# Moving the norm's root from the input to the products, and splitting stage borders into column halves

## The chip, the cores and the metric
One Trainium2 chip, one core. The kernel is one program on one core, with an order of instructions written out by hand for TensorE (matrix products), VectorE, ScalarE and GpSimd, and SyncE for the transfers of the weights. The metric is the device time of one execution in microseconds.

## The reference
Three transformer layers over a sequence of 256 tokens with D = 1024, all in float32. Cut to what matters here:

```
rmsnorm(x, g) = x * rsqrt(mean(x*x) + EPS) * g
layer a:  x += attention(rope(q), rope(k), v) @ w_o   with q, k, v = split(rmsnorm(x) @ w_qkv)
          x += conv_ffn(rmsnorm(x))                   u = h @ w_up; u = conv_b + sum of 3 taps of u; (silu(gate)*val) @ w_down
layer b:  k, v from rmsnorm(x, kv_norm), q from rmsnorm(x, attn_norm[1]), a window of 128 and sinks; then conv_ffn again
          x = rmsnorm(x, final_norm)
layer 2:  xn = rmsnorm(x, norm_mix_pre); proj = xn @ w_in
          a gated delta rule over 8 heads, behind 4-tap convolutions and silus of q, k, v
          retention over 4 heads, behind a rotation
          x += rmsnorm((sigmoid(gate_a)*ya + sigmoid(gate_b)*yb) @ w_out)
          x += rmsnorm(square(relu(rmsnorm(x) @ w_up)) @ w_down)
```

All of it is computed to float32 precision.

## The kernel before
**Weights.** All weights come as 200 units of 1 MB (128 partitions x 2048 values), in the order in which they are used. SyncE loads unit u into one of four raw slots (`load_weights`, L247), as soon as VectorE has finished with unit u-4. ScalarE rounds the unit to a high part in two halves (`hi`, L253, copies at L258 and L259), and VectorE subtracts to get the low part (`lo`, L262, L266 and L268). A product is three matmuls, high x high, low x high, high x low (`three`, L275 to L277). Each engine takes its instructions in the order in which they were written, and the calls of `hi()` and `lo()` stand between the other operations of ScalarE and VectorE at places chosen by hand. `features` (L290) makes a unit's products with features on the partitions, 48 matmuls in four steps; `tokens` (L305) has tokens there.

**Norms.** At every stage border x (256 tokens in two tiles, 1024 columns) gets its residual in four chunks of 128x512 (`residual_dve`, L421, L428), ScalarE sums the squares (`mean_squares_act`, L355), GpSimd makes the root, ScalarE and VectorE scale a tile each into `wide` (L375, L380), TensorE turns it in sixteen 128x128 transposes (L387, `normed_pe`), and ScalarE and VectorE make the high and low part of h from the banks, with the gain (`turn_act` L399, `turn_dve` L411). Then the next stage's products can begin.

**Attention.** `rot_dve` rotates q and k from their bank with the cos and sin tables (L566, L567, L570). In `attn_b` all queries use bank 0, and a query's products wait until the one before is rotated.

**FFN.** 11 laps. A lap has two units up and one down. Per up unit ScalarE applies the newest tap from the bank (`newest_act`, L964) and VectorE the two older taps, four operations (`conv_dve`, L984); then silu (L970), the product (L995), and the high and low part of the gated result (`gate_act` L976, `gate_dve` L999), which the down unit needs (`down_pe`, accumulating in four banks). The scripts of the two engines are `act` (L1001) and `dve` (L1015).

**Delta heads.** 7 laps of `delta_pe`, `delta_act`, `delta_dve`. While TensorE makes the four units of head n = hd+1, head hd's 128x128 inverse is built in six levels: TensorE's `level_a_pe` (L1345), a copy by ScalarE (`level_a_act`, L1351), TensorE's `level_b_pe` (L1356, L1359), a subtraction by VectorE (L1365). `newest_act(n, s)` (L1200) and `older_dve(n, s, back)` (L1208) are the convolution. ScalarE's order around the third level is:

```
newest_act(n, 1)
hi()
level_a_act(hd, 3)
```

and VectorE's `sides_dve(hd)`, `older_dve(n, 1, 1)`, `level_b_dve(hd, 3)`.

**End.** After w_out, `add_normed_dve` (L2117, L2120) adds the normed mix to x, chunk by chunk, and a norm as above leads to the MLP, eight laps of four units.

## Time and profile before

| | us |
|---|---|
| median of 3 runs | 1484.54 |
| lowest, highest | 1483.83, 1486.79 |
| profiled execution, its own time | 1486.77 |
| its span | 1485.2 |
| TensorE busy | 1363.4 |
| VectorE busy | 902.6 |
| ScalarE busy | 726.9 |

All times in the rows are from the profiled execution, counted from the start of its span. The mean granted TensorE clock is 0.972 of full speed. In a timeline row the first number is the start, the second the busy time of the group, and "x4" says how many instructions it holds; the bracket at its end is the time that the engine stood idle before it, and what ended that.

### The profile page before, as it was taken

The numbers are of one execution on the slowest core, as the hardware profiler recorded it, in microseconds if no ns is written. First come the engines' busy times: TensorE is split into PE (matmuls) and PEld (weight loads), VectorE is DVE, ScalarE is ACT, GpSimd is POOL, SyncE is SP. The second block draws the span as 40 slices with busy tenths as digits, with TensorE's granted clock in tenths as the row PEclk, the third lists the DMA queues.
The fourth block names the chain that finished last, engine by engine and source line by source line (L and its number), as shares of the span: only waits on it lengthen the run. The fifth ranks groups of instructions, "written<-read, shape, count | busy, mean of one in ns | idle before, by whom it ended". The sixth has DMA issues, their size and how long they took to land.

```text
span 1485.2 us, 22970 instructions
## 1 busy us (share of the span) xinstructions
PE 1363.4 (92%) x9480; PEld 1241.6 (84%) x9480; DVE 902.6 (61%) x1424; ACT 726.9 (49%) x1260; POOL 88.7 (6%) x145
## 2 busy tenths in 40 slices
PE   6999999987689999978999999979999999699997
PEld 5987999976668999968888888868898877598986
DVE  6765766666557766667666666753557544565553
ACT  6545545554447445557545554543334342553442
POOL 0000000000000000001221221220000000000000
PEclk9999999999899999989999999999999999899999
DMA  8342555433223554433233233223544443365540
GB/s 301 135 167 102 187 202 192 171 142 114 86 85 142 192 203 174 170 139 141 87 114 111 88 115 114 87 84 133 208 151 160 177 168 136 117 248 183 193 142 29
DMA packets 33656, 218.70 MB, mean 147 GB/s; under 512 B 4368, under 2 KB 6032, under 8 KB 7952
## 3 DMA queue, kind: packets, MB, share of 16 engines
q1 hardware_dynamic: 29376, 210.87, 39.2%
q10 hardware_dynamic: 4176, 6.36, 1.3%
q8 instruction: 75, 1.23, 0.3%
q14 instruction: 29, 0.24, 0.1%
HBM read 216.17 MB, written 1.05 MB: 146 GB/s over the span
## 4 chain that ended last, share of the span: by engine, by line
PE 81%; DVE 10%; ACT 5%; issue 2%; POOL 1%; DMA 0%; ACTq 0%; DVEq 0%; SPq 0%; POOLq 0%
PE bank L275 24%; PE bank L276 23%; PE bank L277 23%; DVE sb_w_lo L268 2%; DVE sb_w_lo L266 2%; PE bank L1345 1%; PE bank L1356 1%; ACT sb_w_hi L258 1%; DVE sb_d_xt L1365 1%; PE bank L387 1%; DVE sb_wide L1208 1%; PE bank L643 1%; PE bank L1359 1%; PE bank L592 1%; ACT sb_wide L362 1%
## 5 line engine op out<-in xcount | busy, mean ns | idle before, releaser
L275 PE MATMUL bank<-sb_h_hi,sb_w_hi 128*128 128x256 f32 x1536 | 445.5, 290 | 18.8 <-DVE sb_attn_b_q L570 17.7
L276 PE MATMUL bank<-sb_h_lo,sb_w_hi 128*128 128x256 f32 x1536 | 434.5, 283 | 0.0
L277 PE MATMUL bank<-sb_h_hi,sb_w_lo 128*128 128x256 f32 x1536 | 434.3, 283 | 0.0
L266 DVE TENSOR_TENSOR sb_w_lo<-sb_raw,sb_w_hi 128x1024 fp32r<-128x1024 f32 x200 | 244.3, 1222 | 193.1 <-ACT sb_w_hi L258 192.6
L275 PEld LDWEIGHTS bank<-sb_h_hi,sb_w_hi 128*128 128x128 f32 x1536 | 293.0, 191 | 25.1 <-DVE sb_attn_b_q L570 18.3
L276 PEld LDWEIGHTS bank<-sb_h_lo,sb_w_hi 128*128 128x128 f32 x1536 | 292.9, 191 | 2.7 <-issue 1.4
L277 PEld LDWEIGHTS bank<-sb_h_hi,sb_w_lo 128*128 128x128 f32 x1536 | 292.7, 191 | 0.0
L268 DVE TENSOR_TENSOR sb_w_lo<-sb_raw,sb_w_hi 128x1024 fp32r<-128x1024 f32 x200 | 248.0, 1240 | 0.0
L258 ACT CAST sb_w_hi<-sb_raw 128x1024 fp32r<-128x1024 f32 x200 | 210.3, 1052 | 69.2 <-PE bank L277 69.2
L259 ACT CAST sb_w_hi<-sb_raw 128x1024 fp32r<-128x1024 f32 x200 | 210.8, 1054 | 0.0
L275 PE MATMUL bank<-sb_w_hi,sb_h_hi 128*128 128x256 f32 (+1 forms) x544 | 173.2, 318 | 5.6 <-DVE sb_wide L1208 3.0
L276 PE MATMUL bank<-sb_w_lo,sb_h_hi 128*128 128x256 f32 (+1 forms) x544 | 164.8, 303 | 0.0
L277 PE MATMUL bank<-sb_w_hi,sb_h_lo 128*128 128x256 f32 (+1 forms) x544 | 164.3, 302 | 0.0
L275 PEld LDWEIGHTS bank<-sb_w_hi,sb_h_hi 128*128 128x128 f32 x544 | 103.9, 191 | 11.1 <-DVE sb_wide L1208 3.2
L277 PEld LDWEIGHTS bank<-sb_w_hi,sb_h_lo 128*128 128x128 f32 x544 | 103.6, 190 | 4.6
L276 PEld LDWEIGHTS bank<-sb_w_lo,sb_h_hi 128*128 128x128 f32 x544 | 104.0, 191 | 4.0 <-issue 0.5
L275 PE MATMUL bank<-sb_w_hi,sb_mid_hi 128*128 128x512 f32 (+1 forms) x208 | 82.7, 398 | 6.4 <-DVE sb_attn_b_q L570 6.4
L276 PE MATMUL bank<-sb_w_lo,sb_mid_hi 128*128 128x512 f32 (+1 forms) x208 | 80.8, 388 | 0.0
L277 PE MATMUL bank<-sb_w_hi,sb_mid_lo 128*128 128x512 f32 (+1 forms) x208 | 80.8, 388 | 0.0
L387 PE MATMUL bank<-sb_ident,sb_wide 128*128 128x128 f32 x112 | 23.5, 395 | 43.7 <-ACT sb_wide L375 31.9
L387 PEld LDWEIGHTS bank<-sb_ident,sb_wide 128*128 128x128 f32 x112 | 21.2, 211 | 46.1 <-ACT sb_wide L375 34.1
L984 DVE SCALAR_TENSOR_TENSOR sb_ffn_b_cv<-bank,sb_conv,sb_ffn_b_cv 128x255 f32<-128x255 f32 (+1 forms) x88 | 38.3, 477 | 35.1 <-ACT sb_ffn_b_cv L964 34.4
(310 smaller groups left out, 2001.1 us busy)
## 6 DMA issues: line engine op xcount, KB each, us to landing
sb_raw<-stream SPq DMA_DIRECT2D x200, 1024.0 KB, 4.8
sb_row<-rows ACTq DMA_DIRECT2D x3, 512.0 KB, 4.4
sb_x<-x SPq DMA_DIRECT2D x2, 512.0 KB, 5.4
sb_norm_b<-norm_b ACTq DMA_DIRECT2D x4, 256.0 KB, 3.5
out<-sb_x ACTq DMA_DIRECT2D x4, 256.0 KB, 2.0
sb_retain<-retain ACTq DMA_DIRECT2D x1, 768.0 KB, 4.3
sb_levels<-levels ACTq DMA_DIRECT2D x1, 448.0 KB, 3.3
sb_masks<-mask_full ACTq DMA_DIRECT2D x1, 192.0 KB, 5.3
```

The lines of the kernel that those rows point to most:

```text
L258: A.copy(w_hi[:, b, 0:HALF], raw[:, b, 0:HALF]).then_inc(hi_done, 1)
L259: A.copy(w_hi[:, b, HALF:UNIT], raw[:, b, HALF:UNIT]).then_inc(hi_done, 1)
L266: V.tensor_tensor(w_lo[:, b, 0:HALF], raw[:, b, 0:HALF], w_hi[:, b, 0:HALF].bitcast(F32), ALU.subtract)
L268: V.tensor_tensor(w_lo[:, b, HALF:UNIT], raw[:, b, HALF:UNIT], w_hi[:, b, HALF:UNIT].bitcast(F32), ALU.subtract).then_inc(lo_done, 1)
L275: T.matmul(out_ap, l_hi, r_hi, start=start, stop=False, **kw)
L276: T.matmul(out_ap, l_hi, r_lo, start=False, stop=False, **kw)
L277: return T.matmul(out_ap, l_lo, r_hi, start=False, stop=stop, **kw)
L362: ins = A.activation(chunk(junk, t, n), chunk(x, t, n), ACT.Square, scale=D ** -0.5, accum_out=small[:, 2 * t + n:2 * t + n + 1])
L387: mm = T.transpose(bank[TURN_BANKS[b]][:, c:c + P], wide[:, t, k * P:(k + 1) * P], ident[:])
L592: mm = T.matmul(bank[3 + r][:, c0:c0 + w], self.q[rows, a_, q0:q0 + P], self.k[rows, a_, k0:k0 + w], start=False, stop=a_ == 1, skip_group ...
L643: mm = T.transpose(bank[3 + r][:, c * P:(c + 1) * P], self.sc[:, r, c * P:(c + 1) * P], ident[:])
L984: ins = V.scalar_tensor_tensor(self.cv[:, y, back:S], bank[(0 if j else 2) + s][:, i * S:(i + 1) * S - back], cw[:, y, 2 - back:3 - back], ...
```

## The change
The new kernel turns x as it is, without its norm. The gain is applied where the high and low parts are made; the root r of each token is applied later, to the products. For that a row of the roots is made on every partition: `row_pe` multiplies the broadcast root with the identity (two matmuls), and `row_act` copies the result to `r_row`. Where tokens lie on the partitions the root is a scale of the activation (v, silu_z, the sigmoids); in attention the cos and sin tables are multiplied by the row; in the FFN and in the delta heads each unit's product is multiplied by the row into SBUF ahead of the convolution.

x is turned in two column halves (`turn_x_pe`), the first of them between the last products of the stage before, and the next stage's first two units are interleaved with the second half in `first_two`. The raw slots are three instead of four; the parts of the weights keep four. The queries of attn_b alternate banks 0 and 1, as do the up banks and the gate parts of the FFN and the MLP. In the delta entry the final norm and the pre-norm of the next layer are one root. The core of the diff:

```
-SLOTS = 4
+SLOTS, RAW = 4, 3
...
+                if u >= RAW:
+                    Q.wait_ge(lo_done, u - RAW + 1)
...
+        def row_pe(b, m, c0=4):
+            T.wait_ge(rstd, m + 1)
+            for t in range(NT):
+                mm = T.matmul(bank[b][:, t * P:(t + 1) * P], small[:, c0 + t:c0 + t + 1].to_broadcast([P, P]), ident[:], ...
+        def row_act(b, n):
+            A.wait_ge(row_mm, n + 1)
+            A.copy(r_row[:], bank[b][:, 0:S]).then_inc(row_done, 1)
+        def first_two(u0, b0, u1, b1, fresh, nx, banks, acts=None, second=None):
+            features(u0, b0, 0, acts, fresh)
+            features(u0, b0, 2, acts, fresh)
+            turn_x_pe(nx, 1, banks)
+            second(u1, b1, 0, acts, fresh)
+            second(u1, b1, 2, acts, fresh)
+            features(u0, b0, 1, acts, fresh)
+            features(u0, b0, 3, acts, fresh)
+            second(u1, b1, 1, acts, fresh)
+            second(u1, b1, 3, acts, fresh)
...
         def attn_b_pe(at):
-                T.wait_ge(rot_done, 2 * GROUPS + (1 + g if g else 0))
-                features(q, 0, 0)
+                b, fr = g % 2, 12 if g == 0 else None
+                if g:
+                    T.wait_ge(rot_done, at.rots(g - 2, "q") if o >= 0 else at.rots(0, "k"))
+                features(q, b, 0, fresh=fr)
...
+        def enter_act(mm0, nx, targets, turned_in, h0=0):
+            turn_act(mm0, targets[:1], HALVES[0], turned_in)
+            mean_squares_act(nx, wide)
+            turn_act(mm0, targets[:1], HALVES[1], turned_in)
...
+            def scale_dve(self, j, s):
+                e = 2 * (self.l0 + j) + s
+                V.wait_ge(unit_done, self.up(j, s) + 1)
+                need(V, conv_done, e - 1)
+                V.tensor_tensor(self.ur[:, 2 * s:2 * s + 2, :], bank[self.up_bank(j, s)] ..., r_row ..., ALU.mult).then_inc(up_scaled, 1)
...
-            def act(self):
-                hi(3)
+            def act(self, n):
+                row_act(4, n)
+                hi(2)
                 for j in range(F_LAPS):
                     self.newest_act(j, 0)
                     self.silu_act(j)
                     hi()
                     self.newest_act(j, 1)
-                    if 0 < j < F_LAPS - 1:
-                        hi()
-                    if 0 < j < F_LAPS - 1:
+                    if not last:
                         hi()
                     self.gate_act(j)
-                hi()
+                    if j:
+                        hi()
-            def dve(self, nx, marked):
-                lo(3)
+            def dve(self, n):
+                lo(2)
+                V.wait_ge(row_done, n + 1)
                 for j in range(F_LAPS):
+                    self.scale_dve(j, 0)
                     self.conv_dve(j, 0)
                     lo()
+                    self.scale_dve(j, 1)
                     self.conv_dve(j, 1)
-                    if 0 < j < F_LAPS - 1:
+                    if not last:
                         lo()
                     self.product_dve(j)
-                    if 0 < j < F_LAPS - 1:
+                    self.gate_dve(j)
+                    if j:
                         lo()
-                    self.gate_dve(j)
...
         def newest_act(head, s):
-            A.wait_ge(unit_done, unit_d(head, s) + 1)
+            A.wait_ge(qkv_scaled[s], head + 1)
...
+        def scale_qkv_dve(head, s):
+            V.wait_ge(unit_done, unit_d(head, s) + 1)
+            need(V, conv_d[s], head)
+            V.tensor_tensor(qkv_r[:, 2 * s:2 * s + 2, :], two(bank[s][:, :]), r_row ..., ALU.mult).then_inc(qkv_scaled[s], 1)
         def older_dve(head, s, back):
+            if back == 1:
+                scale_qkv_dve(head, s)
```

At the start ScalarE has the two halves of the turn and two `hi()` ahead of the sums of squares, and `row_act` as the last thing of `begin_act`; VectorE takes `lo()`, the tables, two rotations and then `lo(2)`. In the delta entry the order is `enter_act`, the DMAs, the second sums of squares, `hi()`, `row_act`. After w_out two chunks are added, half 0 is turned, then the other two chunks and half 1. In the MLP the root comes in only with the last norm, through six small operations on GpSimd (`mlp_out_pool`).

## Rows read from the trace of the kernel before

**Rows 1.** The page's first part: busy time, share of the span, instructions.

```profile
PE 1363.4 (92%) x9480; PEld 1241.6 (84%) x9480; DVE 902.6 (61%) x1424; ACT 726.9 (49%) x1260; POOL 88.7 (6%) x145
```

**Rows 2.** Waits of TensorE: who for whom, us in total, times, longest.

```profile
PE bank L387 <- ACT sb_wide L375: 31.9, 5, 11.2
PE bank L275 <- DVE sb_attn_b_q L570: 24.1, 4, 8.3
...
PE bank L275 <- DVE sb_wide L1208: 3.0, 1, 3.0
```

**Rows 3.** Stretches in an FFN, attn_b, a delta head, the MLP.

```profile
core 0: us, PE busy (x) PEld busy (x) DVE busy (x) ACT busy (x) POOL busy (x), PEclk, DMA share, GB/s
138.00:325.00 187.00, 187.00 (x1325) 175.09 (x1324) 131.36 (x186) 102.21 (x141) 0.00 (x0) 1.00 0.51 184
345.00:421.00 76.00, 51.88 (x408) 46.25 (x406) 38.25 (x93) 30.03 (x86) 0.00 (x0) 0.84 0.23 84
818.00:859.00 41.00, 38.01 (x307) 36.54 (x306) 26.61 (x53) 21.45 (x46) 9.14 (x12) 1.00 0.29 104
1300.00:1475.00 175.00, 175.00 (x1108) 157.59 (x1108) 89.32 (x83) 74.32 (x88) 0.00 (x0) 1.00 0.45 162
```

**Rows 4.** Groups by line and shape: total busy, mean ns | idle before, releaser.

```profile
L362 ACT ACTIVATE sb_wide<-sb_x 128x512 f32<-128x512 f32 x24 | 15.0, 627 | 27.8 <-DVE sb_x L428 20.7 <-DVE sb_x L1103 3.7 <-DMA sb_x<-x 3.4
L2103 ACT ACTIVATE sb_junk<-bank 128x512 f32<-128x512 f32 x8 | 4.7, 595 | 27.4 <-PE bank L277 27.4
...
L984 DVE SCALAR_TENSOR_TENSOR sb_ffn_a_cv<-bank,sb_conv,sb_ffn_a_cv 128x255 f32<-128x255 f32 x44 | 19.1, 476 | 33.5 <-ACT sb_ffn_a_cv L964 33.5
L2117 DVE SCALAR_TENSOR_TENSOR sb_wide<-bank,sb_small,sb_row 128x512 f32<-128x512 f32 x8 | 6.0, 746 | 28.5 <-POOL sb_small L347 28.5
L566 DVE TENSOR_TENSOR sb_attn_a_cosp<-bank,sb_cos_t 128x512 f32<-128x512 f32 x8 | 5.5, 683 | 0.0
L1103 DVE SCALAR_TENSOR_TENSOR sb_x<-sb_x,sb_small,sb_row 128x512 f32<-128x512 f32 x4 | 2.7, 746 | 2.2 <-POOL sb_small L347 2.2
L457 DVE SCALAR_TENSOR_TENSOR sb_sin_t<-sb_turns,sb_pos_f 128x256 f32<-128x256 f32 x1 | 0.4, 425 | 0.0
```

**Rows 5.** Timeline of VectorE in one FFN lap.

```profile
179.78 1.77 DVE L984 SCALAR_TENSOR_TENSOR sb_ffn_a_cv<-bank,sb_conv,sb_ffn_a_cv 128x255 f32<-128x255 f32 x4
181.47 1.22 DVE L266 TENSOR_TENSOR sb_w_lo<-sb_raw,sb_w_hi 128x1024 fp32r<-128x1024 f32 x1
...
183.74 0.69 DVE L995 TENSOR_TENSOR sb_ffn_a_sg<-sb_ffn_a_sg,sb_ffn_a_cv 128x512 f32<-128x512 f32 x1
...
191.03 1.78 DVE L984 SCALAR_TENSOR_TENSOR sb_ffn_a_cv<-bank,sb_conv,sb_ffn_a_cv 128x255 f32<-128x255 f32 x4 [3.74 <-ACT sb_ffn_a_cv L964]
```

**Rows 6.** Timeline of ScalarE in the next lap.

```profile
189.98 1.02 ACT L964 ACTIVATE sb_ffn_a_cv<-bank,sb_conv 128x256 f32<-128x256 f32 x2 [4.90 <-PE bank L277]
192.85 0.63 ACT L970 ACTIVATE sb_ffn_a_sg<-sb_ffn_a_cv 128x512 f32<-128x512 f32 x1 [1.85 <-DVE sb_ffn_a_cv L984]
```

**Rows 7.** Timeline of ScalarE at the start.

```profile
24.60 1.03 ACT L258 CAST sb_w_hi<-sb_raw 128x1024 fp32r<-128x1024 f32 x1
```

**Rows 8.** Timeline of TensorE at two stage borders.

```profile
135.40 3.30 PE L387 MATMUL bank<-sb_ident,sb_wide 128*128 128x128 f32 x16 [3.65 <-ACT sb_wide L375]
...
1290.82 3.67 PE L387 MATMUL bank<-sb_ident,sb_wide 128*128 128x128 f32 x16 [11.18 <-ACT sb_wide L375]
```

**Rows 9.** Timeline of TensorE in attn_b, before and after a wait.

```profile
364.63 0.28 PE L275 MATMUL bank<-sb_h_hi,sb_w_hi 128*128 128x256 f32 x1
364.74 0.28 PE L276 MATMUL bank<-sb_h_lo,sb_w_hi 128*128 128x256 f32 x1
...
372.42 0.58 PE L275 MATMUL bank<-sb_h_hi,sb_w_hi 128*128 128x256 f32 x1 [7.28 <-DVE sb_attn_b_q L570]
372.80 0.41 PE L276 MATMUL bank<-sb_h_lo,sb_w_hi 128*128 128x256 f32 x1
373.01 0.41 PE L277 MATMUL bank<-sb_h_hi,sb_w_lo 128*128 128x256 f32 x1
```

**Rows 10.** Timelines of ScalarE, VectorE and TensorE in one delta head.

```profile
865.55 0.84 ACT L1200 ACTIVATE sb_wide<-bank,sb_conv_a 128x256 f32<-128x256 f32 x2
869.53 0.37 ACT L1351 COPY sb_d_zm<-bank 128x256 f32<-128x256 f32 x1 [1.25 <-PE bank L1345]
868.78 0.87 DVE L1208 SCALAR_TENSOR_TENSOR sb_wide<-bank,sb_conv_a,sb_wide 128x255 f32<-128x255 f32 x2
870.75 0.61 PE L1356 MATMUL bank<-sb_d_zm,sb_d_xt 128*128 128x128 f32 x4
```

**Rows 11.** Timeline of GpSimd after the last squares.

```profile
1476.47 0.19 POOL L346 TENSOR_TENSOR sb_small<-sb_small,sb_pool_const 128x2 f32<-128x2 f32 x1
1476.75 0.70 POOL L347 TENSOR_TENSOR sb_small<-sb_small,sb_pool_const 128x2 f32<-128x2 f32 x1
```

More of the change, by code:

```diff
@@ L574, in v_act @@
                 need(A, pv_done, GH * (self.g0 + g))
-                A.copy(self.v[:].rearrange("p a n -> p (a n)"), bank[2][:, :]).then_inc(v_copied, 1)
+                for t in range(NT):
+                    ins = A.activation(self.v[:, t, :], bank[2][:, t * 256:(t + 1) * 256], ACT.Copy, scale=small[:, 4 + t:5 + t])
+                ins.then_inc(v_copied, 1)
             def scores_pe(self, g):
@@ L765, in attn_b_pe @@
                     at.values_pe(o, PAIRS[1])
-                features(q, 0, 3)
+                features(q, b, 3)
         def attn_b_act(at):
-            hi(3)
+            row_act(7, 2)
+            hi(2)
             at.v_act(0)
@@ L806, in two_tiles @@
             for k in range(2):
-                mm = three(bank[2 * n + t][:, :], mid_hi[:, k0 + k, tk], mid_lo[:, k0 + k, tk],
+                mm = three(bank[banks[n][t]][:, :], mid_hi[:, k0 + k, tk], mid_lo[:, k0 + k, tk],
                            wh[:, k, nn], wl[:, k, nn], False, k0 + k == KD - 1)
@@ L882, in wo_act, with wo_dve @@
             at.keep_act(g)
-            hi()
-        def wo_dve(at, nx, marked, name):
+            hi(2)
+        def wo_dve(at, marked, name, banks, h0, gain):
             g = GROUPS - 1
@@ L913, in __init__ @@
                 self.parts = [[sb(f"{name}_{p}_{b}", [P, 2, S], F32R, scope=scope) for p in ("hi", "lo")]
-                              for b in ("all", "last")]
+                              for b in ("even", "odd")]
                 self.scope = scope
@@ L1082, in two @@
             return ap.rearrange("p (a n) -> p a n", a=NT)
+        R0, NR0, R1 = 50, 54, 52
+        root = [small[:, R0 + t:R0 + t + 1] for t in range(NT)]
         def delta_begin_act():
-            mean_squares_act(4, wide)
+            A.wait_ge(mask_ready, 1)
+            enter_act(16, 4, [(8, h_hi, h_lo)], AFTER_FFN)
             for dst, src in ((upper[:], a["upper"]), (lower[:], a["lower_strict"]),
@@ L1147, in gates_act @@
             A.wait_ge(gate_mm, 1)
-            A.activation(beta, ba_ps[:, :, 0:A_HEADS], ACT.Exp, scale=-1.0).then_inc(beta_exp, 1)
+            for t in range(NT):
+                ins = A.activation(beta[:, t, :], ba_ps[:, t, 0:A_HEADS], ACT.Exp, scale=small[:, NR0 + t:NR0 + t + 1])
+            ins.then_inc(beta_exp, 1)
             A.activation(log_bias[:, 0, :], log_bias[:, 0, :], ACT.Exp)
@@ L1207, in older_dve @@
                 y = 2 * s + i
-                ins = V.scalar_tensor_tensor(cv[:, y, back:S], bank[s][:, i * S:(i + 1) * S - back],
+                ins = V.scalar_tensor_tensor(cv[:, y, back:S], qkv_r[:, y, 0:S - back],
                                              cw[:, y, 3 - back:4 - back], cv[:, y, back:S], ALU.mult, ALU.add)
@@ L1220, in keep_v_act @@
             A.wait_ge(unit_done, unit_d(head, 2) + 1)
-            A.copy(v_ret[:, :, head * 256:(head + 1) * 256], two(bank[0][:, :])).then_inc(v_ret_done, 1)
+            for t in range(NT):
+                ins = A.activation(v_ret[:, t, head * 256:(head + 1) * 256], bank[0 if head else 2][:, t * 256:(t + 1) * 256],
+                                   ACT.Copy, scale=root[t])
+            ins.then_inc(v_ret_done, 1)
         def silu_z_act(head):
@@ L1225, in silu_z_act @@
             need(A, o_gated, head)
-            A.activation(zs[:].rearrange("p a n -> p (a n)"), bank[2][:, :], ACT.Silu).then_inc(zs_done, 1)
+            for t in range(NT):
+                ins = A.activation(zs[:, t, :], bank[2][:, t * 256:(t + 1) * 256], ACT.Silu, scale=root[t])
+            ins.then_inc(zs_done, 1)
         def flip_qk_pe(hd):
@@ L1657, in sig_act @@
             for t in (1, 0):
-                A.activation(chunk(wide, t, n), bank[banks[t]][:, :], ACT.Sigmoid).then_inc(sig_a, 1)
+                A.activation(chunk(wide, t, n), bank[banks[t]][:, :], ACT.Sigmoid, scale=root[t]).then_inc(sig_a, 1)
         def gate_a_pe():
@@ L1931, in gsl_act @@
                 need(A, ob_gated, hd)
-                A.activation(gsl[:, :, j * 256:(j + 1) * 256], two(bank[2 + j][:, :]), ACT.Silu).then_inc(gsl_done[j], 1)
+                for t in range(NT):
+                    ins = A.activation(gsl[:, t, j * 256:(j + 1) * 256], bank[2 + j][:, t * 256:(t + 1) * 256], ACT.Silu,
+                                       scale=root[t])
+                ins.then_inc(gsl_done[j], 1)
         def retention_pe():
@@ L2046, in gate_b_act @@
                 for t in range(NT):
-                    A.activation(chunk(sig, t, n), bank[2 * n + t][:, :], ACT.Sigmoid).then_inc(sig_b, 1)
+                    A.activation(chunk(sig, t, n), bank[2 * n + t][:, :], ACT.Sigmoid, scale=root[t]).then_inc(sig_b, 1)
             hi()
```

564 lines of the change are left out of this document (303 added, 261 removed).

## The prediction
> **What bounds the kernel now.** I read the page's busy shares first: TensorE works in 92% of the span [rows 1], so at most the other 8% can be won without less TensorE work. The waits of TensorE come next [rows 2]: 31.9 us in five waits for the scaled x (L375), 24.1 us in four waits for the rotated query of attn_b, 3.0 us for a convolution in the delta entry. The table of stretches says where there is nothing to win [rows 3]: in the FFN TensorE works without a break, in a delta head 38.0 of 41.0 us, in attn_b only 51.9 of 76. So the change can win at most some 60 us at stage borders and in attn_b, and whatever it puts on VectorE or ScalarE inside the FFN and the heads has to be held against their chains, not their busy shares. I went through these with the timelines.
>
> The profiled execution took 1486.8 us (span 1485.2); the sum below is a difference and is added to the median, 1484.5.
>
> **Durations.** An element-wise VectorE operation on 128x512 takes 0.68 to 0.69 us, a tap 0.48, four taps 1.77, a `lo` pair start to start 2.27 [rows 4, 5]; `newest` 1.02, silu 0.63 [rows 6]; a half copy of `hi` 1.03 to 1.07 [rows 7]; sixteen transposes 3.30 [rows 8].
>
> **FFN laps.** Before, TensorE needs 16.95 us a lap (three units of 5.65), and VectorE has slack: before the first taps of a lap it stands 3.7 us [rows 5]. The change adds two 128x512 multiplications (`scale_dve`), but also turns free-standing work into one chain: unit done, scale, `newest` on ScalarE, taps, silu on ScalarE, `hi` behind silu, `lo`, scale, `newest`, taps, `lo`, product, gate copy on ScalarE, `gate_dve`, third `hi`, third `lo`, and VectorE takes all of it in this order. Start to start: 0.72 + 1.06 + 1.82 + 1.60 (silu and a first `hi` half) + 2.28 + 0.72 + 1.06 + 1.69 + 2.27 + 0.72 + 0.66 + 0.94 (the third `hi` begins only after the gate copy) + 2.28 = 17.8 us. That is over 16.95: nine full laps each grow by 0.87, +7.8. What isn't in the trace is taps that read SBUF instead of a bank. Rows differ on whether that is cheaper: ScalarE takes 0.63 from SBUF and 0.60 from a bank on 128x512, VectorE's scalar_tensor_tensor 0.746 from either [rows 4]; but one with constants reads 128x256 of SBUF in 0.425 against 0.477 for a tap. By the first the chain stays, by the second eight taps give back 0.4 and it is 17.4; if other hand-overs shorten too, laps are at TensorE's 16.95. I take 17.8, since the 0.746 rows carry a register operand as the taps do.
> The Trainium skill (Perfetto Trace Analysis, Optimizing Scalar/DVE Operations) gives a fixed access cost per instruction that is about 65 ns smaller for VectorE on SBUF than on PSUM, and some 40 ns larger for ScalarE. By it, as an estimate, the lap would be 17.8 - 8 x 0.065 + 4 x 0.04 = 17.4, and the two FFNs 7 us shorter than I sum; the trace has the ScalarE side (0.63 against 0.60) and not VectorE's (0.746 in both).
>
> **FFN entry and end.** T is the end of the output projection. Before: 3.65 us idle, 3.30 us of transposes [rows 8], then no wait, so that down(0) begins at T+29.5. Now half of the transposes stand ahead of T (T itself is 1.65 later), features begin at T+0.3, the other half and the two first units in `first_two` end at T+13.4, and `row_pe` (0.45) follows. But `act` now begins with `row_act`, and only behind it comes `hi(2)`: the third unit's weights start at T+14.4 and are whole (copy half, `lo` pair) at T+17.8. TensorE waits 3.9 us. VectorE takes `lo(2)` ahead of its first scale, at T+20.1 instead of `newest` at T+13.6, and needs 15.2 from there to the first gate part: down(0) at T+35.3, another wait of 6.2. With the later T: +7.4. At the end down(10) follows down(9)'s gate by 13.1 us of chain instead of 5.65 us of product: +7.5. One FFN: 7.4 + 7.8 + 7.5 = **+22.7**. For the second 22.9, as in wo_b chunks also wait in another order (T +2.8 instead of +1.65, its entry being the same otherwise). Between: 0 if the entry is hidden and laps are TensorE's, +28 if the chain is 0.5 longer.
>
> **Start.** x arrives un-normed at once, features begin at 14.2 instead of 16.3 (-2.1). But ScalarE has the turn of half 0, `hi`, turn of half 1 (which waits for transposes that now stand behind unit 0's first steps), and only then `hi` of unit 1: +4.8 of waiting. Mean squares, nine DMA issues, the sine and `row_act` come before `hi(3)`, which began at 24.60 [rows 7] and now begins at about 33: +3.9 for v; the tables times the row and two rotations ahead of `lo(2)`: +1.9; `row_pe` 0.45. Sum **+8.9** (+4 if the sine isn't late, +12 if the DMAs crowd the weights).
>
> **ffn_a to attn_b.** The wait for L375 (3.6), and slow transposes go; unit q0 waits again for its weights behind `row_act` (3.9). k and v finish earlier: **-3.0** (0 to -6).
>
> **attn_b.** Before, query g waits until query g-1 is rotated, which waits for the softmax of its neighbour: 24.1 us in four waits [rows 2]. With banks in turns the wait is for g-2, done a lap earlier. What is late next is the softmax itself before its transposes, as long as one unit of 5.65: laps of 14.6 instead of 19 to 21. After such a wait products also start slow, 0.21 us apart against 0.12 [rows 9]. From q0 to the third scores 73.7 becomes 49.9: **-23.8** (-15 to -27).
>
> **Delta entry.** The waits of 9.9 and 3.0 go. But between `first_two` and the head's rows come the second norm: x times gain, squares, a chain on GpSimd with two roots, 0.70 each [rows 11], `row_act`, then the gates with their table loads, and the last weights behind `keep_v_act`. I find TensorE idle for 14 us: **+1.7**, and +1 for products at the low clock after it. Bounds -8 to +10.
>
> **Delta heads.** `newest_act(n, 1)` ran at 865.55 [rows 10], straight from the bank. Now it waits for `scale_qkv_dve`, which VectorE takes at the place of `older_dve(n, 1, 1)`, 868.78, later by the first scale and what that delays (to about 870.5). On ScalarE, `hi()` (two copies) and `level_a_act(hd, 3)`, which ran at 869.53, stand behind it: 870.5 + 0.7, `newest` 0.84, two copies 1.9, copy 0.37 = 873.6 at the earliest for level_b(3) on TensorE, which ran at 870.75 [rows 10]. The levels go one by one, so nothing gives it back: 2.8 x 7 = **+19.8**. Bounds: 0 if VectorE reaches the scale by 867.5, +30.
>
> **w_out to the MLP.** 11.2 us idle and 3.7 us of slow transposes now [rows 8]. The halves let TensorE begin the first unit at about 1287.5 instead of 1294.15; transposes and slow products take some back: **-4.3** (-2 to -8). The MLP itself (175 of 175 us busy [rows 3]) has no scale, since its root is in the last norm; alternate banks win nothing there. The last chain on GpSimd has three small operations more at 0.27 each [rows 11]: **+0.8**. gate_a and retention: silus in two parts and two table products, **+1**.
> **Raw slots.** A unit's transfer is now issued one `lo` later. In laps its 1 MB has over 10 us; I cost it 0 (up to +5 where `hi` come in bursts).
>
> Sum: 8.9 + 22.7 - 3.0 - 23.8 + 22.9 + 2.7 + 19.8 - 4.3 + 0.8 + 1.0 = +47.7, that is **1532 us**.
>
> **Rivals.**
> A, FFN laps stay TensorE's. For it: SBUF sources may be cheaper; against it: cheaper taps give back 0.4 of the 0.87. Then the laps' 7.8 and a little of the last lap go, twice: +29, 1513.
> B, the head's shift is hidden as well, because the scale on VectorE comes before the level's subtraction does. +9, 1493.
> C, faster: the gaps close and nothing replaces them. Place: ScalarE's queue at the stage entries and VectorE's in the laps. It decides if the row is ready before TensorE has used its two prefetched units (row at T+8 instead of T+13.9) and a lap's chain is below 16.95: of the 31.9 us some 20 go, 24 in attn_b, 3 in the delta entry; transposes and row products add 3: -44, 1440; with half of that 1462. Against it: `row_pe` stands behind both units in TensorE's order, so the row can't come earlier.
> D, three raw slots bind: transfers in bursts add 0.5 us to each lap of both FFNs and to branches, 15 in all: 1547.
>
> **Numbers.** My sum 0.50 (own range 1518 to 1548), A 0.16, B 0.10, C 0.18, D 0.06. The range that leaves 2 in 10 out: 1478 to 1553. Less than 0.2% (3 us) can't be told from no change here: faster 0.20, same 0.03, slower 0.77.
>
> **What would show it.** Right: TensorE waits of some 4 us for `w_lo` in both FFN entries, then some 6 for the gate's low part; laps of 17.8 in the FFN with TensorE waits for `lo`; the waits for attn_b_q gone; in a head, ScalarE standing before `newest_act(n, 1)` for about 5 us and level_b(3) 2.8 later, with the head's period at 44.0; GpSimd's last chain 0.8 longer. Wrong: FFN laps at 16.95 (A), head period 41.2 (B), no wait for `w_lo` at entries (C), or queue waits of weights for a slot with TensorE behind them (D).

## The result and the profile after

| | us |
|---|---|
| before, median (lowest to highest) | 1485.66 (1483.83 to 1486.80) |
| after, median | 1560.24 (1553.65 to 1560.88) |
| ratio, 95% interval | 1.0493 (1.0462 to 1.0525) |
| span of the profiled execution, before and after | 1485.2, 1559.3 |

The change costs 75 us. The forecast was 1532, its range ended at 1553: the direction was right, the sum 28 us short. One of the four executions of after_start2 below took 5648 us and counts as slow; every ratio compares fast executions alone. First the page of the new kernel, whose first line answers to [rows 1]; TensorE is 25 us longer busy for nearly the same instructions (9500 matmuls against 9480).

```profile
PE 1388.9 (89%) x9500; PEld 1257.8 (81%) x9500; DVE 944.9 (61%) x1479; ACT 730.4 (47%) x1283; POOL 93.9 (6%) x152
...
PE 57%; DVE 24%; ACT 11%; issue 6%; POOL 1%; DMA 1%; ACTq 0%; DVEq 0%; POOLq 0%
```

The second line is the chain that ended last, by engine. In the kernel before it read PE 81%, DVE 10%, ACT 5%. The share that left TensorE went for the most part to VectorE and ScalarE, although the busy share of VectorE is 61% in both: a sign of hand-overs, not of load. The waits of TensorE answer to [rows 2]:

```profile
PE bank L276 <- DVE sb_w_lo L269: 30.0, 6, 9.8
PE bank L276 <- DVE sb_ffn_b_lo_even L1087: 16.8, 5, 10.0
PE bank L276 <- DVE sb_ffn_a_lo_even L1087: 16.2, 5, 10.0
PE bank L1478 <- ACT sb_d_zm L1473: 15.7, 10, 2.3
PE bank L1467 <- DVE sb_d_xt L1487: 15.3, 16, 1.2
PE bank L1392 <- DVE sb_small L1379: 11.5, 1, 11.5
PE bank L1430 <- ACT sb_wide L1425: 7.2, 7, 1.5
PE bank L382 <- DMA sb_gains<-gains: 6.3, 1, 6.3
PE bank L681 <- DVE sb_attn_b_sc L674: 5.7, 4, 2.5
```

The waits for the scaled x and for the rotated query are gone, and others have their places: six for the weights' low part, ten for the gate's (even half; six more of under 1 us for the odd), ScalarE's copy in the heads (L1478) and, once a head, a wait ahead of the head's products (L1430). Stretches against [rows 3]: the FFN, attn_b, a delta head, and ten microseconds within that head.

```profile
184.00:340.00 156.00, 151.36 (x1058) 140.47 (x1059) 112.14 (x158) 79.57 (x105) 0.00 (x0) 0.99 0.49 175
383.00:460.00 77.00, 67.96 (x530) 56.11 (x530) 57.90 (x131) 44.83 (x122) 0.00 (x0) 0.93 0.34 121
842.00:888.50 46.50, 40.80 (x304) 39.00 (x305) 28.00 (x54) 21.67 (x49) 9.90 (x12) 0.93 0.26 91
890.00:900.00 10.00, 8.38 (x46) 8.22 (x47) 5.70 (x8) 1.98 (x6) 1.37 (x1) 0.66 0.29 105
```

Since both kernels make the same 200 units of weights in the same order, the start of each unit's second `lo` half on VectorE is a good ruler. The kernel after minus the one before, us: unit 0 2.6; unit 9 16.9; unit 15 17.4; unit 48 (the last lap of ffn_a) 30.8; unit 51 38.8; unit 57 15.7; unit 90 35.6; unit 96 (delta entry) 41.9; unit 126 (last head) 77.6; unit 168 78.4; unit 180 73.8; unit 198 73.2. The loss was made at the start, in both FFNs and in the heads, and attn_b gave 23 back.

**One FFN lap**, VectorE, to be held against [rows 5]:

```profile
238.36 0.68 DVE L1063 TENSOR_TENSOR sb_ffn_a_ur<-bank,sb_r_row 128x512 f32<-128x512 f32 x1
240.21 1.79 DVE L1072 SCALAR_TENSOR_TENSOR sb_ffn_a_cv<-sb_ffn_a_ur,sb_conv,sb_ffn_a_cv 128x255 f32<-128x255 f32 x4 [1.17 <-ACT sb_ffn_a_cv L1045]
243.63 1.22 DVE L267 TENSOR_TENSOR sb_w_lo<-sb_raw,sb_w_hi 128x1024 fp32r<-128x1024 f32 x1 [1.64 <-ACT sb_w_hi L259]
...
245.91 0.68 DVE L1063 TENSOR_TENSOR sb_ffn_a_ur<-bank,sb_r_row 128x512 f32<-128x512 f32 x1
247.76 1.79 DVE L1072 SCALAR_TENSOR_TENSOR sb_ffn_a_cv<-sb_ffn_a_ur,sb_conv,sb_ffn_a_cv 128x255 f32<-128x255 f32 x4 [1.17 <-ACT sb_ffn_a_cv L1045]
...
253.12 0.69 DVE L1087 TENSOR_TENSOR sb_ffn_a_lo_even<-sb_ffn_a_sg,sb_ffn_a_hi_even 128x512 fp32r<-128x512 f32 x1 [0.69 <-ACT sb_ffn_a_hi_even L1056]
254.07 1.22 DVE L267 TENSOR_TENSOR sb_w_lo<-sb_raw,sb_w_hi 128x1024 fp32r<-128x1024 f32 x1 [0.26 <-ACT sb_w_hi L259]
```

Every bracket names ScalarE and none names TensorE: VectorE never waits for a product, and its five idle gaps, 1.17 + 1.64 + 1.17 + 0.69 + 0.26 = 4.9 us, are four hand-overs to ScalarE and back and one copy. Steady laps are 17.98 us apart (before 16.95). TensorE does not feel this at once: its second to fourth down products still come 16.78 us apart, and only from the sixth on does it keep VectorE's step, with a wait of 0.9 us in each lap. The lag is paid at the last down product, whose matmuls then run at the low clock (0.79 and 0.63 us for a matmul of 128x512, against 0.40 at 364.07):

```profile
359.65 0.79 PE L276 MATMUL bank<-sb_w_hi,sb_ffn_a_hi_even 128*128 128x512 f32 x1 [10.04 <-DVE sb_ffn_a_lo_even L1087]
361.09 0.63 PE L276 MATMUL bank<-sb_w_hi,sb_ffn_a_hi_even 128*128 128x512 f32 x1
...
364.07 0.40 PE L276 MATMUL bank<-sb_w_hi,sb_ffn_a_hi_even 128*128 128x512 f32 x1
```

The entry has the two waits of TensorE that were forecast, of 3.8 and 3.9 us; the second had been put at 6.2:

```profile
166.92 0.58 PE L276 MATMUL bank<-sb_h_hi,sb_w_hi 128*128 128x256 f32 x1 [3.80 <-DVE sb_w_lo L269]
184.55 0.50 PE L276 MATMUL bank<-sb_w_hi,sb_ffn_a_hi_even 128*128 128x512 f32 x1 [3.91 <-DVE sb_ffn_a_lo_even L1087]
```

Taps from SBUF aren't cheaper, and `newest` is dearer by 33 ns (594 against 561), by group:

```profile
L1072 DVE SCALAR_TENSOR_TENSOR sb_ffn_a_cv<-sb_ffn_a_ur,sb_conv,sb_ffn_a_cv 128x255 f32<-128x255 f32 x44 | 19.4, 481 | 25.6 <-ACT sb_ffn_a_cv L1045 25.6
...
L1045 ACT ACTIVATE sb_ffn_a_cv<-sb_ffn_a_ur,sb_conv 128x256 f32<-128x256 f32 x44 | 24.1, 594 | 45.4 <-DVE sb_ffn_a_ur L1063 45.4
```

A tap takes 481 ns against 476 [rows 4]. The rule of the Trainium skill that I had weighed (Perfetto Trace Analysis, Optimizing Scalar/DVE Operations) is borne out for ScalarE (some 40 ns stated, 33 measured) and not for VectorE's taps (65 ns less stated, 5 more measured).

**A delta head**, ScalarE, VectorE and TensorE, against [rows 10]:

```profile
887.57 0.91 ACT L1308 ACTIVATE sb_wide<-sb_d_qkv_r,sb_conv_a 128x256 f32<-128x256 f32 x2 [3.92 <-DVE sb_d_qkv_r L1315]
888.38 1.03 ACT L259 CAST sb_w_hi<-sb_raw 128x1024 fp32r<-128x1024 f32 x1
...
890.27 0.36 ACT L1473 COPY sb_d_zm<-bank 128x256 f32<-128x256 f32 x1
...
886.84 0.69 DVE L1315 TENSOR_TENSOR sb_d_qkv_r<-bank,sb_r_row 128x512 f32<-128x512 f32 x1
...
890.68 0.71 PE L1478 MATMUL bank<-sb_d_zm,sb_d_xt 128*128 128x128 f32 x4 [1.77 <-ACT sb_d_zm L1473]
892.77 1.20 PE L1467 MATMUL bank<-sb_d_xt,sb_d_low_b 128*128 128x128 f32 x4 [0.94 <-DVE sb_d_xt L1487]
...
919.98 0.71 PE L1430 MATMUL bank<-sb_wide 128*128 128x128 f32 x4 [0.94 <-ACT sb_wide L1425]
```

ScalarE stands 3.9 us before `newest_act(n, 1)`, the copy of the level is behind it in its queue, and TensorE waits 1.8. What follows at once was in no step of mine: the clock. In the ten microseconds from 890 the granted clock is 0.66 (above), and the same work in the kernel before had 1.00. Four matmuls of a level take 1.20 us, instead of 0.68 in the kernel before, where the same wait of 0.94 stands ahead of them:

```profile
872.75 0.68 PE L1345 MATMUL bank<-sb_d_xt,sb_d_low_b 128*128 128x128 f32 x4 [0.94 <-DVE sb_d_xt L1365]
```

It is not so in every head. The second of the seven has the same waits, 1.78 and 0.94, and keeps the full clock:

```profile
799.07 0.71 PE L1478 MATMUL bank<-sb_d_zm,sb_d_xt 128*128 128x128 f32 x4 [1.78 <-ACT sb_d_zm L1473]
798.00:810.00 12.00, 9.90 (x80) 9.45 (x80) 7.73 (x10) 5.01 (x9) 0.76 (x1) 1.00 0.24 89
```

The levels serve as a ruler within a head. From the first `level_b_pe` of a head to that of the next, over seven heads, the new kernel takes 32.4 us more than the old: 13.9 up to the third level, where the new wait is (1.9 to 2.5 in six of the heads, 1.7 in the first); 11.4 from the third to the sixth, where there is no new wait and the clock differs (0.5 of it is there at the full clock too, in after_scale_early); 7.0 from the sixth to the next head's first, with the new wait at L1430.

**The start:**

```profile
6.25 1.97 PE L382 MATMUL bank<-sb_ident,sb_x 128*128 128x128 f32 x8 [6.25 <-DMA sb_gains<-gains]
17.98 0.58 PE L276 MATMUL bank<-sb_h_hi,sb_w_hi 128*128 128x256 f32 x1 [9.76 <-DVE sb_w_lo L269]
28.39 0.46 PE L276 MATMUL bank<-sb_h_hi,sb_w_hi 128*128 128x256 f32 x1 [4.77 <-DVE sb_w_lo L269]
42.95 0.58 PE L276 MATMUL bank<-sb_w_hi,sb_h_hi 128*128 128x256 f32 x1 [3.90 <-DVE sb_w_lo L269]
...
13.29 0.29 DVE L539 CAST sb_pos_f<-sb_pos_i 128x256 f32<-128x256 int32 x1 [13.29 <-DMA sb_pos_i<-positions]
```

The second and third waits are the ones forecast (4.8 and 3.9). The first products came at 17.98, not at 14.2. VectorE's first instruction is the positions' conversion, and their transfer, now fourth in ScalarE's queue, landed at 13.3 us (before at 7.9); the low part of h and of the weights stood behind it. After each of the three waits the products come 0.21 us apart at first: 24 of them take 4.6, 4.5 and 5.3 us, where 2.8 is the steady time and the first 24 of the kernel before take 3.1. The end of GpSimd's chain has six operations instead of three, as forecast [rows 11]; two of them:

```profile
1549.78 0.20 POOL L2234 TENSOR_TENSOR sb_small<-sb_small 128x2 f32<-128x2 f32 x1
1550.05 0.20 POOL L2235 TENSOR_TENSOR sb_small<-sb_small 128x2 f32<-128x2 f32 x1
```

### The profile page after: what moved, and what is told of

It is laid out like the page before. It is cut to its first block, busy times and chain, and to the rows that moved or that the text cites. A ratio compares the mean times of both kernels' runs of the same rounds, so it can differ in the third digit from the quotient of the medians.

```text
span 1559.3 us, 23153 instructions
## 1 busy us (share of the span) xinstructions
PE 1388.9 (89%) x9500; PEld 1257.8 (81%) x9500; DVE 944.9 (61%) x1479; ACT 730.4 (47%) x1283; POOL 93.9 (6%) x152
## 4 chain that ended last, share of the span: by engine, by line
PE 57%; DVE 24%; ACT 11%; issue 6%; POOL 1%; DMA 1%; ACTq 0%; DVEq 0%; POOLq 0%
PE bank L276 16%; PE bank L277 16%; PE bank L278 16%; DVE sb_w_lo L269 6%; DVE sb_w_lo L267 5%; ACT sb_w_hi L259 4%; DVE sb_ffn_b_cv L1072 2%; DVE sb_ffn_a_cv L1072 2%; DVE sb_d_xt L1487 1%; PE bank L1478 1%; PE bank L1467 1%; ACT sb_ffn_a_cv L1045 1%; ACT sb_ffn_b_cv L1045 1%; POOL sb_small L348 1%; PE bank L681 1%
## 5 line engine op out<-in xcount | busy, mean ns | idle before, releaser
L276 PE MATMUL bank<-sb_w_hi,sb_h_hi 128*128 128x256 f32 (+1 forms) x544 | 178.7, 329 | 6.7 <-DVE sb_w_lo L269 3.9
L277 PE MATMUL bank<-sb_w_lo,sb_h_hi 128*128 128x256 f32 (+1 forms) x544 | 170.2, 313 | 0.0
L278 PE MATMUL bank<-sb_w_hi,sb_h_lo 128*128 128x256 f32 (+1 forms) x544 | 169.7, 312 | 0.0
L276 PEld LDWEIGHTS bank<-sb_w_hi,sb_h_hi 128*128 128x128 f32 x544 | 109.1, 201 | 12.1 <-DVE sb_w_lo L269 4.1
L278 PEld LDWEIGHTS bank<-sb_w_hi,sb_h_lo 128*128 128x128 f32 x544 | 108.7, 200 | 4.6
L277 PEld LDWEIGHTS bank<-sb_w_lo,sb_h_hi 128*128 128x128 f32 x544 | 109.2, 201 | 4.0 <-issue 0.5
L1487 DVE TENSOR_TENSOR sb_d_xt<-sb_d_xt,bank 128x512 f32<-128x512 f32 (+1 forms) x48 | 30.7, 640 | 59.4 <-PE bank L1481 37.5
L1461 POOL TENSOR_TENSOR sb_d_low_b<-sb_d_low,sb_levels 128x256 f32<-128x256 f32 x48 | 45.6, 957 | 151.0 <-PE bank L1467 90.9
L1072 DVE SCALAR_TENSOR_TENSOR sb_ffn_b_cv<-sb_ffn_b_ur,sb_conv,sb_ffn_b_cv 128x255 f32<-128x255 f32 (+1 forms) x88 | 38.7, 481 | 26.4 <-ACT sb_ffn_b_cv L1045 25.6
```

What stands on the lines that cost most here:

```text
L276: T.matmul(out_ap, l_hi, r_hi, start=start, stop=False, **kw)
L277: T.matmul(out_ap, l_hi, r_lo, start=False, stop=False, **kw)
L278: return T.matmul(out_ap, l_lo, r_hi, start=False, stop=stop, **kw)
L1072: ins = V.scalar_tensor_tensor(self.cv[:, y, back:S], self.ur[:, y, 0:S - back], cw[:, y, 2 - back:3 - back], self.cv[:, y, back:S], ALU.m ...
L1461: G.tensor_tensor(low_b[:, b % 2], low[:], levels[:, b:b + 1, :].to_broadcast([P, NT, P]), ALU.mult).then_inc(blocks_done, 1)
L1487: V.tensor_tensor(xt[:, 0:w, :], xt[:, 0:w, :], bank[7][:, 0:w * P].rearrange("p (a n) -> p a n", n=P), ALU.subtract).then_inc(inv, 1)
```

## The experiments

All times are medians; each comes beside runs of the kernel before on the same chip (1484.9 to 1486.6), the ratio with its interval is to these. "Gain" is against after's 1560.2. The four executions of after lie 7 us apart and the interval of its ratio is worth 4.7 us either side, so a gain of under 5 us is read with the ruler of the units and not from the medians.

**before_banks and before_raw3**, one part of the change each, in the kernel before. before_banks also has the banks of the change in the output projection behind attn_b; its core:

```
-                T.wait_ge(rot_done, 2 * GROUPS + (1 + g if g else 0))
-                features(q, 0, 0)
+                T.wait_ge(rot_done, 2 * GROUPS if g == 0 else at.rots(g - 2, "q") if o >= 0 else at.rots(0, "k"))
+                features(q, g % 2, 0)
```

> The kernel before with one edit of the change: the queries of attn_b alternate banks 0 and 1, and the output projection behind it uses banks in the change's order. My account (the bank is what the query waits for): all 24.1 us of waits for the rotated query go, some come back as waits for the softmax, -20 to -24 us, 1462 to 1466. Rival (the banks only seem to matter, the softmax chain sets the pace of attn_b): the waits move to the transposes of the softmax and the gain is under 8 us, above 1477.

Measured 1461.4, ratio 0.9841 (0.9826 to 0.9856): -23.8 us. That this is the term of the forecast to its decimal is luck, since the interval is 2.2 us either side; that the waits were the bank's is shown. The waits for the query are gone, and 5.7 us in four for the softmax stand in their place:

```profile
PE bank L643 <- DVE sb_attn_b_sc L636: 5.7, 4, 2.5
```

> The kernel before with three raw slots instead of four, nothing else. My account: 0 (within 1 us), since a unit's transfer is issued a lap ahead and lands in about 5 us. Rival D of the prediction (three slots bind, and explain the loss that I missed): +10 us or more, with TensorE waits for the weights' low part, mostly at the start and in the branches.

Measured 1484.4, ratio 1.0000 (0.9990 to 1.0009). In the new kernel ScalarE's `hi` copies stand 0.5 us in all for a weight transfer. Rival D is out.

**after_hi_first**: the copies ahead of the row, two units in both FFNs and in attn_b, one at the start. The FFN's part:

```
             def act(self, n):
-                row_act(4, n)
                 hi(2)
+                row_act(4, n)
```

> The kernel after with ScalarE's hi copies put ahead of row_act: hi(2) ahead of it in both FFNs and in attn_b, one hi() ahead of it at the start. My account (the weights queue behind the row): the three waits of 3.8 to 3.95 us for the low part go and the row's users come earlier; -5.6 in each FFN, -3.9 in attn_b, up to -3.9 at the start, -15 to -19 in all, about 1543. Rival (the row itself is late, so whatever waits for it waits as long): the waits move to the first gate part and to the rotation, and the gain is under 6.

Measured 1538.2, ratio 1.0365 (1.0344 to 1.0386): gain 22, against 15 to 19 of my account. By the ruler 4.4 us come at the start, 5.4 at the entry of ffn_a, 4.7 at attn_b and 5.6 at ffn_b, 20 in all, each close to its forecast. In the entry of ffn_a the wait of 3.8 for the weights is gone, that for the first gate part is 4.6 instead of 3.9:

```profile
PE bank L276 <- DVE sb_ffn_a_lo_even L1088: 4.6, 1, 4.6
```

**after_ffn_order and after_ffn_unscaled**: what makes the lap long, the work or its order.

```
                     self.scale_dve(j, 0)
-                    self.conv_dve(j, 0)
                     lo()
-                    self.scale_dve(j, 1)
-                    self.conv_dve(j, 1)
-                    if not last:
-                        lo()
+                    self.conv_dve(j, 0)
+                    self.scale_dve(j, 1)
+                    if not last:
+                        lo()
+                    self.conv_dve(j, 1)
```

On ScalarE `hi()` goes ahead of `newest_act(j, 0)`, and the second `hi()` ahead of `newest_act(j, 1)`.

> The kernel after with the FFN's order changed alone: on VectorE each of the first two lo pairs stands between scale and taps instead of behind the taps, on ScalarE hi stands ahead of newest. The same instructions, the same scaling. My account (the lap is a chain of hand-overs, 17.98 us against TensorE's 16.95, and its last lap pays the lo pairs): VectorE's idle time is filled, laps fall to 16.95 (-1.0 x 9), the wait before the last down product (10.0) falls to about 1, the first to about 2: -20 an FFN, 1520. Rival (the two added multiplications make the lap too long by their own time): laps stay near 17.9 and the gain is under 8.

Measured 1512.0, ratio 1.0173 (1.0137 to 1.0209): gain 48, where 40 were expected.

> The kernel after without the FFN's multiplication by the row (it leaves the root out of both FFNs): newest and the taps read the bank as in the kernel before, the order of everything else is after's. My account: the chain of a lap is shorter by the two multiplications and their two hand-overs, 0.72 each, 17.98 - 1.44 = 16.5, so laps are TensorE's 16.95: -1.0 x 9 an FFN; the waits before the first and the last down product lose 1.4 each; -24 in all, about 1536. Rival (the order alone, with three lo pairs behind one another, makes the loss): laps stay above 17.5, gain under 10. Rival (taps from SBUF are cheaper by 0.065 each, so leaving SBUF costs 0.5 a lap): laps still 16.95, but the last wait shrinks by under 1.

Measured 1508.9, ratio 1.0147 (1.0114 to 1.0179): gain 51. So leaving the multiplications out brings no more, as far as can be told (3 us, and the intervals overlap), than keeping them all and moving `lo`. In after_ffn_order TensorE has no break from 184 to 320, with VectorE busier than in after (110 us against 97 of these 136):

```profile
184.00:320.00 136.00, 136.00 (x969) 127.26 (x969) 110.20 (x152) 76.19 (x102) 0.00 (x0) 1.00 0.55 194
```

My account holds in its mechanism, and for after_ffn_unscaled its size was half (24 expected): I took the last wait to shrink by the shortened chain (1.4 us), but in a loop that the chain bounds, that wait is lag, and it is gone as soon as the loop is TensorE's. The waits in ffn_a for the gate's low part fall from 19.0 us to 2.0 (after_ffn_order) and 0.9 (after_ffn_unscaled). Besides, such laps are 16.78 us, not 16.95 (below).

**after_scale_early and after_scale_both**: the heads.

```
             lo()
+            scale_qkv_dve(n, 1)
             if first:
                 store_dve(hd - 1)
```

In after_scale_both, on ScalarE, `newest_act(n, 0)` also stands behind `second_values_act` and `back_qk_act`.

> The kernel after, in the delta heads alone: VectorE multiplies unit (n,1) by the row straight behind the lo pair ahead of store_dve, not behind sides_dve. Seven heads each lost 5.2 us, of which TensorE's new waits are 1.8 at level_b(3) and 0.9 at the products; some 2.2 more is matmuls at the low clock behind the first of them (granted clock 0.66 from 890 to 900). Theory 1 (that wait is the cause, and the low clock its consequence): the 1.8 wait and the 2.2 go, and the clock stays 1.00 there: -4 a head, -26 to -28 in all, about 1532. Theory 2 (the low clock comes with the waits of 0.9 that stay, or with the altered order): only the wait goes, -1.8 a head, -12, about 1547.

Measured 1535.5, ratio 1.0338 (1.0323 to 1.0354): gain 24.7. By the levels 13.8 of it are the wait and what it delayed, and 10.9 the clock. The granted clock of a whole head is 1.00 again, though both waits of 0.94 stay, the old one between the levels and the new one ahead of the products:

```profile
843.00:885.00 42.00, 38.10 (x306) 36.39 (x305) 28.25 (x55) 21.94 (x48) 9.43 (x12) 1.00 0.28 99
```

> As after_scale_early, and on ScalarE newest_act(n,0) stands behind second_values_act and back_qk_act, which it delayed. Theory 1: the waits of 0.9 before the products go as well, -6 to -7 more than after_scale_early, about 1526. Rival: older_dve(n,0,1) comes later and delays low_dve, so the levels start as late as before: no further gain.

Measured 1527.5, ratio 1.0285 (1.0268 to 1.0303): gain 32.7. Steady heads are 41.23 us apart (before 41.18, after 44.4 to 47.2), and the 7.0 us from the sixth level to the next head are gone. The loss between one head and the next was two places in two queues; the multiplications themselves cost 0.05 us a head. Theory 1 stands: the low clock comes with the wait of 1.8, in six heads of seven, and not with those of 0.94 alone. That the wait causes it is shown in so far as taking it away restored the clock in every head; why one head kept its clock isn't.

**after_pos_late, after_start2, after_start3**: the start, one step further each. VectorE's part of the last:

```
         def begin_dve():
-            V.wait_ge(tables_in, 32)
-            (positions and their two operations)
             turn_dve(0, ..., HALVES[0], FOUR)
-            lo()
+            lo(2)
             turn_dve(0, ..., HALVES[1], FOUR)
-            lo()
+            lo(2)
+            V.wait_ge(tables_in, 32)
+            (positions and their two operations)
```

after_pos_late moves the positions alone; after_start2 has lo(2) and lo(), after_start3 lo(2) and lo(2), with hi to match and so many fewer later.

> The kernel after, at the start alone: VectorE's wait for the positions and the two operations on them stand behind its second lo, not ahead of everything. The positions landed at 13.3 us, and VectorE's low part of h waited for them. My account: first features at 14.5 instead of 17.98, and -3.5 to -5 in all, since nothing behind gives it back. Rival (the sine and the row are on the path at the start, and they come later now): v's weights wait longer by as much, gain under 1.

Measured 1556.5, ratio 1.0476 (1.0461 to 1.0492): gain 3.7, less than the noise of a median. The trace shows it: the first products come at 14.24 instead of 17.98, and the units ahead of the heads 3.6 us earlier.

```profile
14.24 0.58 PE L276 MATMUL bank<-sb_h_hi,sb_w_hi 128*128 128x256 f32 x1 [5.90 <-DVE sb_w_lo L269]
```

> The kernel after, at the start alone: the edit of after_pos_late, and both engines take unit 1's weights (hi(2), lo(2)) ahead of the second half of the turn and unit 2's straight behind it, ahead of the squares, the sine and the row. Measured so far at the start: waits of 9.8, 4.8 and 3.9 us for the low part. My account (all three are places in a queue): the second goes, the third goes, the first falls by 3.5; -3.5 - 4.8 - 3.9 = -12 at most, less 2 to 3 that the row's users (tables, rotations) take back: -9 to -12, about 1549. Rival (the row is late, the first rotation and with it q of group 1 wait as before): under 6.

Measured 1555.4, ratio 1.0474 (1.0456 to 1.0491): gain 4.8, not 9 to 12. The two waits are gone, and a new one for unit 3's weights stands at 41.18, of 6.0 us.

```profile
41.18 0.55 PE L276 MATMUL bank<-sb_h_hi,sb_w_hi 128*128 128x256 f32 x1 [5.96 <-DVE sb_w_lo L269]
```

> The kernel after, at the start alone: as after_start2, and unit 3's weights are taken ahead of the sine, the tables and the two rotations as well (hi(2), lo(2) behind the second half of the turn). In after_start2 the waits of 4.8 and 3.9 us went, but a new one of 6.0 us stood at 41.2, for unit 3's low part, which VectorE made behind the tables and the rotations, and these behind sine and row. Theory 1 (it is the place of the lo in VectorE's queue): that wait goes, -5 us against after_start2, 1550. Theory 2 (the row and the sine themselves are late, whatever is queued around them): the wait moves to the first rotation or to unit 4's weights and the gain is under 2.

Measured 1548.4, ratio 1.0437 (1.0416 to 1.0459): gain 11.8, 7 more than after_start2. The wait that is left here is 2.7 us for the rotated query, which needs sine and row:

```profile
14.17 0.58 PE L276 MATMUL bank<-sb_h_hi,sb_w_hi 128*128 128x256 f32 x1 [5.90 <-DVE sb_w_lo L269]
28.78 0.71 PE L426 MATMUL bank<-sb_ident,sb_small 128*128 128x128 f32 x4 [0.77 <-POOL sb_small L348]
37.88 0.55 PE L276 MATMUL bank<-sb_h_hi,sb_w_hi 128*128 128x256 f32 x1 [2.72 <-DVE sb_attn_a_q L606]
```

The medians mislead about both. Against after, the ruler has these differences (us), and the heads are the same code in all four kernels:

| | unit 9 | unit 96, ahead of the heads | unit 126, last head |
|---|---|---|---|
| after_pos_late | -4.6 | -3.6 | -7.1 |
| after_start2 | -7.7 | -8.7 | -5.8 |
| after_start3 | -11.3 | -11.1 | -15.1 |

So the edit of after_start2 is worth 8 to 9 us at the start, a little under my account and over the rival's 6, and the step to after_start3 2.4 to 3.6 and not 7. The rest is made in the heads, where nearly the same six waits for the level's copy (11.8 us in all in after_start2, 10.7 in after_start3) were followed by the low clock more often in one execution than in the other. Six laps of heads in each, after_start2 first:

```profile
770.00:1046.00 276.00, 243.00 (x1805) 230.75 (x1804) 168.30 (x320) 129.72 (x279) 54.84 (x70) 0.94 0.26 92
767.00:1037.00 270.00, 236.97 (x1809) 224.39 (x1808) 168.02 (x321) 129.85 (x281) 56.43 (x70) 0.97 0.27 94
```

Of the wait of 6.0 us theory 1 (the place of the `lo`) explains the 3.2 that went, theory 2 (row and sine are late) the 2.7 that are left.

**after_all4 and after_all6**: the edits together.

> The edits of after_hi_first, after_ffn_order, after_scale_both and after_pos_late together. Alone they gave 22, 48, 33 and 4 us. Both of the first act on the FFN's first down product, so some 8 should be lost: 1560 - 107 + 8 = 1461. If the parts don't add (another bound, TensorE's own work or the weights), it is above 1475.

Measured 1458.4, ratio 0.9822 (0.9806 to 0.9838). The parts add up; its four executions lie 0.6 us apart, with the full clock in all heads.

> The edits of after_all4 with the start of after_start3. By theory 1 5 to 6 us under after_all4 (1458.4), 1453; by theory 2 1457 to 1459.

Measured 1455.6, ratio 0.9802 (0.9787 to 0.9816), the fastest here: 29 us below the kernel before, 105 below after, with all of the change's arithmetic. The start gives 3 us of its expected 5 there, and by the ruler 2.6, as in after_start3. Most of these 29 us are not the norm's: alternate banks in attn_b alone gave 23.8, and the rest of the change in its best order adds some 6. In the FFNs 22 laps of 16.78 instead of 16.95 us make 3.7 of the 6 by an estimate, and why such laps are shorter is open (below). The same with the start of after_start2, **after_all5**, is no different from after_all4:

> As after_all4 with the start of after_start2: if start's 9 to 12 hold against 4 of after_pos_late and the 3.9 that after_hi_first has there already, 2 to 4 us under after_all4, 1457 to 1459, and so under the kernel before with alternate banks alone (1461).

Measured 1459.3, ratio 0.9824 (0.9810 to 0.9839).

**before_flags and before_upbanks**: why two units of products take 11.21 us in every kernel with the change and 11.36 in the one before. before_flags sets one start flag for each bank in `features`, before_upbanks alternates the up banks of FFN and MLP over four.

> The kernel before with one start flag for each bank in features instead of one for each half of it, as after has it; nothing else. In after, two units of 48 matmuls of 128x256 take 11.21 us in the FFN and the MLP, in before 11.36, which no step of the prediction has. If the flag does it: pairs of units at 11.21, 48 of them or so, about -7 us, 1478. If the alternating banks do it: no change, 1485.

Measured 1485.5, ratio 0.9994 (0.9985 to 1.0003); pairs at 11.36.

> The kernel before with the up products of FFN and MLP alternating over four banks, and waiting for the lap before the last; nothing else. If alternating does it (a product no longer goes into a bank that was just read): pairs at 11.21 in 30 laps, about -4 us, 1481. If the flag does it: no change, 1485, as the prediction had it (nothing in the MLP waited for a bank).

Measured 1484.5, ratio 0.9991 (0.9982 to 1.0000); pairs at 11.36. Neither does it, nor do attn_b's banks or three raw slots: pairs are at 11.36 in before_banks and before_raw3 too. Down units, which have another shape, differ as well (5.57 against 5.59). Alternating the up banks is worth nothing by itself, as forecast, within 3 us, and the cause of the 0.15 us stays open.

## Why the prediction was wrong

By its terms, against the ruler of the units and the runs:

| term | forecast | measured |
|---|---|---|
| start | +8.9 | +17 |
| ffn_a, to the start of down(10) | +22.7 | +22.7 |
| ffn_a to attn_b and attn_b | -26.8 | -24 |
| wo_b and ffn_b | +22.9 | +23 |
| delta entry | +2.7 | +3 |
| delta heads | +19.8 | +36 |
| gate_a and retention | +1.0 | +0.3 |
| w_out and MLP | -4.3 | -5 |
| end | +0.8 | +0.8 |

(ffn_a: down(10) began at 359.65 against 319.6, 40.1 later, of which 17.4 are the start. Delta entry and heads: `row_decay_pe` began at 723.85, 42 later than before, and the last head's units came 78 later. Of the 36 us of the heads 3.4 lie ahead of the first head's levels.)

- **The FFN lap** was right in size and cause: chain 17.8 forecast, 17.98 measured; bound by hand-overs. The choice between the rows on taps was the right one. That the FFN as a whole came out at +22.7 to the decimal is luck: the entry cost 5.6 and not 7.4, with a second wait of 3.9 and not 6.2; the laps 6.6 and not 7.8, since the first of them stayed TensorE's; the end 10.4 and not 7.5. Rival A, that laps stay TensorE's, is out for this order of `lo`, and holds for the other.
- **Weights behind the row**: forecast 3.9 us for v and at each entry, measured 3.8 to 3.95, and confirmed by after_hi_first.
- **attn_b** was right, alone (-23.8) and in the change.
- **Delta heads, the step that failed.** "2.8 x 7" had the place and the queue right: `newest_act(n, 1)` waits (3.9 us, about 5 forecast), `level_a_act(hd, 3)` is late behind it, and nothing gives that back, so rival B is out. But it costed only this wait, and that at the full clock. Measured over the seven heads, the third level comes 13.9 us later, less than the 19.8 of the sum. (By its own terms, 870.5 + 0.7 + 0.84 + 1.9 + 0.37, level_b(3) would be at 874.3 and not at 873.6, so the term was too large by still more.) On top of it came two costs that the sum has at nothing: the low clock behind the wait, 10.9 us in six heads of the seven, and 7.0 us at the products ahead of the next head's levels (L1430), which `newest_act(n, 0)`, late behind its own multiplication, makes wait. The prediction knew the effect of the clock (it costed it in attn_b, from [rows 9]) and did not apply it here. For the first multiplication it reckoned only with what it delays on the way to the second.
- **Start, the second.** I followed ScalarE's queue and not VectorE's first instruction. The positions' transfer stood second in ScalarE's DMA queue and now stands fourth, and VectorE's queue begins with its wait: 3.8 us (14.2 forecast, 17.98 measured; after_pos_late gives 3.6 of it back). The other 5.6 us are slow products behind the three waits, 0.21 us apart as in [rows 9], for which the sum has no term here. The 1.9 for tables and rotations ahead of `lo(2)` did not appear as a wait of its own: unit 3's weights are in time here, and are late only in after_start2. 8.9 + 3.8 + 5.6 - 1.9 is 16.4 of the measured 17.
- **Rival C** (1440 if nothing replaced the gaps) was wrong for this order, but not for this change: with the queues in another order it is at 1455.6, between C's two times of 1440 and 1462.
- **Range.** Terms of known mechanism added up to 47.7 with rivals mostly on the low side. The high end held no term for the low clock behind the new waits at the start and in seven heads.

## What to carry to other kernels

An operation that is added between a product and its consumer costs its place, not its time: where it stands behind something slow in one queue, all that stands behind its consumer in the next queue pays. Before adding it, write out both engines' orders and ask for each hand-over what fills it; a pair of copies that wait for nobody, moved into it, was worth 48 us here, against 51 for deleting the work. Cost every new wait of TensorE twice, once for its length and once for the products behind it if the clock falls, the second as a range (here in six heads of seven). Where the clock scatters like this in one stretch, read the gain of an edit elsewhere from the trace ahead of that stretch. And count an engine's first instruction among the things that a moved transfer can delay.
